# A two-block transformer kernel: the second norm's first steps made beside the first block's output projection, and weight totals asked for one group later

## What is computed

```
x = layer_norm(x, ln_in_g, ln_in_b)
h = einsum('bsd,de->bse', x, w_in[l])
...                                    # the three mixers: ya, yb, yc
y = einsum('bse,ed->bsd', concatenate([ya, yb, yc], -1), w_out[l])
x = layer_norm(DEEPNORM_ALPHA * x + y, post_ln_g[l], post_ln_b[l])      # x1

h = rmsnorm(x, norm_pre_g)             # y = xf * rsqrt(mean(xf*xf) + eps) * g
z = einsum('bsd,de->bse', h, w_in)
...                                    # rope, three dilated window attentions, gates, a convolution
y = einsum('bse,ed->bsd', mixed, w_out)
x = x + rmsnorm(y, norm_post_g)
```

## Time and profile before

| | |
|---|---|
| median of 3 runs | 2297.74 us (2291.33 to 2300.5) |
| profiled execution | 2291.84 us |
| its span, first to last instruction | 2289.7 us |
| mean granted TensorE clock | 0.962 |
| busy: PE, DVE, ACT, POOL | 91%, 61%, 40%, 40% |
| PE idle ahead of line 236, five single waits | 2.67, 2.72, 2.76, 2.67, 4.34 us |
| last projection matmul to first dense matmul of the second norm | 920.35 to 955.32 us |

### The profile page before, as it was taken

How to read it: one execution, slowest core, us unless ns; L and a number is a source line. 1 busy time by engine, 2 the same in 40 slices (tenths; PEclk the granted TensorE clock), 3 DMA queues, 4 the chain that set the end, 5 groups by cost and what they waited for, 6 DMA issues and landing times.

```text
span 2289.7 us, 43310 instructions
## 1 busy us (share of the span) xinstructions
PE 2082.4 (91%) x16228; PEld 1525.7 (67%) x16228; DVE 1394.7 (61%) x3507; ACT 923.1 (40%) x1981; POOL 906.7 (40%) x1004
## 2 busy tenths in 40 slices
PE   5999999997898999499999999999988888887998
PEld 3545868886787888488644444656877766666786
DVE  7614949765897444773376772213179999994422
ACT  3323333222796000232233431211179999883111
POOL 4311333363422999332111211211132888983222
PEclk9999999998899999799999999999999999997999
DMA  5441321346633232442344431321156787674552
GB/s 180 134 110 57 108 80 44 92 142 201 154 80 107 79 109 98 156 135 66 115 118 137 117 116 49 117 73 55 49 123 161 195 197 185 169 220 135 161 172 90
DMA packets 285536, 279.95 MB, mean 122 GB/s; under 512 B 39712, under 2 KB 237216, under 8 KB 285072
## 3 DMA queue, kind: packets, MB, share of 16 engines
q1 hardware_dynamic: 281280, 271.08, 41.1%
q0 software_dynamic: 1680, 5.51, 0.6%
q10 hardware_dynamic: 2368, 0.60, 0.1%
HBM read 171.22 MB, written 93.31 MB: 116 GB/s over the span
## 4 chain that ended last, share of the span: by engine, by line
PE 27%; DVE 16%; issue 4%; ACT 2%; POOL 2%; DMA 2%; SPq 1%; DVEq 0%; ACTq 0%; POOLq 0%
PE bank L172 19%; PE bank L2507 7%; DVE s2m L2357 6%; DVE p2l L2363 4%; DMA qr<-qf 1%; DVE qf L1801 1%; SPq L1830 1%; ACT s2sh L1781 1%; DVE qr L1799 1%; DVE s2sl L1804 1%; DVE qf L1798 1%; DVE ob L2369 1%; PE bank L2302 1%; POOL qs L2399 0%; ACT p2r L2336 0%
## 5 line engine op out<-in xcount | busy, mean ns | idle before, releaser
L172 PE MATMUL bank<-xh,w2l 128*128 128x512 f16 x640 | 244.7, 382 | 0.0
L172 PE MATMUL bank<-xh,w2h 128*128 128x512 f16 x640 | 244.5, 382 | 0.0
L172 PE MATMUL bank<-xl,w2h 128*128 128x512 f16 x640 | 244.5, 382 | 0.0
L172 PE MATMUL bank<-w1h,xh 128*128 128x256 f16 x768 | 212.6, 277 | 3.0 <-DVE s1st L918 3.0
L172 PE MATMUL bank<-w2h,xh 128*128 128x256 f16 x768 | 211.3, 275 | 2.0 <-issue 2.0
L2302 PE MATMUL bank<-ident,p2r 128*128 128x128 f32 x900 | 165.9, 297 | 51.9 <-DVE p2l L2363 45.7
L172 PE MATMUL bank<-w1l,xh 128*128 128x256 f16 x768 | 212.5, 277 | 0.0
L172 PE MATMUL bank<-w1h,xl 128*128 128x256 f16 x768 | 212.4, 277 | 0.0
L172 PE MATMUL bank<-w2h,xl 128*128 128x256 f16 x768 | 211.2, 275 | 0.0
L172 PE MATMUL bank<-w2l,xh 128*128 128x256 f16 x768 | 211.2, 275 | 0.0
L2302 PEld LDWEIGHTS bank<-ident,p2r 128*128 128x128 f32 x900 | 97.4, 145 | 108.5 <-DVE p2l L2363 105.7
(11 more groups left out here) (345 smaller groups left out, 5643.1 us busy)
## 6 DMA issues: line engine op xcount, KB each, us to landing
scr_part<-ob SPq DMA_DIRECT2D x48, 264.0 KB, 3.2
cm<-scr_part SPq DMA_DIRECT2D x48, 264.0 KB, 4.7
v<-scr_v SPq DMA_DIRECT2D x192, 65.0 KB, 2.6
w2r<-in_w_in SPq DMA_DIRECT2D x12, 1024.0 KB, 6.4
qr<-qf SPq DMA_DIRECT2D x192, 64.0 KB, 2.0
ax<-in_x SPq DMA_DIRECT2D x16, 512.0 KB, 5.3
xr<-in_x SPq DMA_DIRECT2D x16, 512.0 KB, 4.4
bx<-scr_x SPq DMA_DIRECT2D x16, 512.0 KB, 6.2
```

The lines of the kernel that those rows point to most:

```text
L172: ins = nc.tensor.matmul(dst, x, y, start=k == 0 and m == 0, stop=k == n - 1 and m == 2)
```

## The change

Four things. (1) The second norm's gain scale, the load, statistics and scaling of its first four row tiles, and its first weight chunk's load, square, total and scale are made in `project_stage`, between tiles 5 and 15, in tiles of their own (`rows2`, `raw2`, `junk2`). ACT scales the rows, not DVE. (2) The stores of x1 are left out of the take-over; row loads wait for the stores of their own rows. All engines take over first and then begin. (3) In both norms the totals of chunks 2 and 3 stand one dense group later. (4) In the gate stage the total stands behind the fourth tile of a chunk, not the second, and the scaling one tile later. Chunk 2 of the second norm no longer shares its buffer with chunk 0, so its load doesn't wait for it. The core of the diff:

```diff
-        handed_over = hand_over() if late else ()
+        handed_over = hand_over(ahead["stores"]) if late else ()
...
-        if late:
-            sb(f"{tag}pad", [128, 17000], scope=scope)
...
-        work = [("wide",), ("load", 0)]
+        work = [] if late else [("wide",), ("load", 0)]
...
             if g == 1:
-                work += [("load", 2), ("total", 2)]
+                work.append(("load", 2))
+            if g == 2:
+                work.append(("total", 2))
...
-        work += [("consts",), ("load", 3), ("total", 3)]
-        work += [("group", 2, 0), ("scaled", 3)] + [("group", 2, g) for g in range(1, 4)]
+        work += [("consts",), ("load", 3)]
+        work += [("group", 2, 0), ("total", 3), ("group", 2, 1), ("scaled", 3), ("group", 2, 2), ("group", 2, 3)]
...
-                elif x_ready is not None:
-                    sp.wait_ge(*x_ready[t])
+                if late:
+                    sp.wait_ge(*ahead["stored"][4 * g + t])
...
-                    pe.wait_ge(*d_sc.at(4 * g + 4))
+                    pe.wait_ge(*(ahead["scaled"] if late and g == 0 else d_sc.at(4 * (g - off) + 4)))
...
         def dve_program():
-            if not keep:
-                dve_most()
-                dve_widest()
+            take_over(dve)
+            if not late:
+                dve_scale(0)
                 dve_widened()
-            dve_scale(0)
-            if keep:
-                dve_widened()
-            take_over(dve)
...
         def sp_program():
-            sp_fetch(0)
             take_over(sp)
-            wts.sp_load(0)
+            if not late:
+                sp_fetch(0)
+                wts.sp_load(0)
             wts.sp_load(1)
...
     # project_stage
+            if n == 8:
+                wide_bank = tbk.take(d_wd.at(5))
+            if n == 13:
+                total_bank = tbk.take(d_wt.at(1))
+        def sp_ahead(n):
+            if n == 6:
+                nc.sync.dma_start(raw2[:], ...).then_inc(*w_in.up(16))
+            if 8 <= n < 12:
+                t = n - 8
+                sp.wait_ge(*x_out[t].at(16))
+                nc.sync.dma_start(rows2[t][:], x1[128 * t:128 * t + 128, :]).then_inc(*n_in[t].up(16))
+        def dve_ahead(n):            # behind dve_residual(n + 2)
+            if n == 5:
...                                  # four small operations on the gain
+            elif n == 8:
+                dve.wait_ge(*p_wd.at(1))
+                nc.vector.tensor_scalar(whole, wide_bank[0][:, 0:1], 1e-30, None, ALU.max).then_inc(*d_wd.up())
+            elif n == 11:
...                                  # two small operations
+            if 10 <= n < 14:
+                t = n - 10
+                dve.wait_ge(*n_in[t].at(16))
...                                  # bn_stats x2, bn_aggr of rows2[t]
+            elif n == 14:
...                                  # three small operations
+            if n == 13:
+                dve.wait_ge(*p_wt.at(1))
+                nc.vector.tensor_scalar(size2[:, 0, 1:2], total_bank[0][:, 0:1], 1e-30, None, ALU.max).then_inc(*d_wt.up())
+        def act_ahead(n):            # behind ACT's copies of tile n
+            if n == 10:
+                act.wait_ge(*w_in.at(16))
+                nc.scalar.activation(junk2[:], raw2[:], ACT.Square, accum_out=size2[:, 0, 0:1]).then_inc(*a_ws.up())
+            elif n == 15:
+                act.wait_ge(*g_nx.at(1))
+                for t in range(4):
+                    nc.scalar.activation(rows2[t][:], rows2[t][:], ACT.Identity, scale=rs2[:, t:t + 1]).then_inc(*a_nx.up())
+        def pool_ahead(n):           # behind POOL's power of tile n
...                                  # n == 10: three small operations; n == 13: five; n == 14: one power of four columns
     # PE, round n, behind pe_turn(n + 1)
+                if n == 7:
+                    nc.tensor.matmul(wide_bank[0][:, 0:1], ones_[:], own, start=True, stop=True).then_inc(*p_wd.up())
+                if n == 12:
+                    nc.tensor.matmul(total_bank[0][:, 0:1], ones_[:], size2[:, 0, 0:1], start=True, stop=True).then_inc(*p_wt.up())
...
     # gate_stage
-                    if len(tiles) % 8 == 2 and first + n + 1 < len(wts.chunks):
+                    if len(tiles) % 8 == 4 and first + n + 1 < len(wts.chunks):
...
-                if m % 8 == 1 and x["n"] in total_bank:
+                if m % 8 == 3 and x["n"] in total_bank:
                     wts.pe_total(first + x["n"] + 1, *total_bank[x["n"]])
...
-                if m % 8 == 4 and first + m // 8 + 1 < len(wts.chunks):
+                if m % 8 == 5 and first + m // 8 + 1 < len(wts.chunks):
                     wts.act_scale(first + m // 8 + 1)
...
-                if m % 8 == 2 and x["n"] in total_bank:
+                if m % 8 == 4 and x["n"] in total_bank:
                     wts.dve_total(first + x["n"] + 1, total_bank[x["n"]][0])
```

More of the change, by code:

```diff
@@ L184, in __init__ @@
             self.lo = sbs(f"{tag}l", 2, [128, 8, 256], FH, scope)
-            self.size = sb(f"{tag}z", [128, len(chunks), 4], scope=scope)
+            self.size = sb(f"{tag}z", [128, len(chunks), 4], scope=scope) if first is None else first["size"]
             self.un = [un[:, block, n:n + 1] for n in range(len(chunks))]
@@ L192, in __init__ @@
             at, dma_at = [None, self.a_w.n, self.d_w.n, self.g_w.n], [x.n for x in self.dma]
[L193 to L196, removed]
+            done = 0 if first is None else 1
+            self.summed = [(self.a_n, self.a_n.n + n + 1 - done) for n in range(len(chunks))]
+            self.added = [(self.p_t, self.p_t.n + n + 1 - done) for n in range(len(chunks))]
+            self.total = [(self.d_t, self.d_t.n + n + 1 - done) for n in range(len(chunks))]
+            self.scaled = [(self.g_u, self.g_u.n + 5 * (n - done) + 5) for n in range(len(chunks))]
+            if first is not None:
+                self.scaled[0] = first["scaled"]
             self.landed, self.by_act, self.half, self.ready = [], [], [], []
+            self.first = first
             for n, c in enumerate(chunks):
-                dma_at[n % 2] += 16 * len(c["cols"])
+                dma_at[n % 2] += 16 * len(c["cols"]) if n or first is None else 0
                 at[1] += 1
-                self.landed.append((self.dma[n % 2], dma_at[n % 2]))
+                self.landed.append((self.dma[n % 2], dma_at[n % 2]) if n or first is None else first["landed"])
                 self.by_act.append((self.a_w, at[1]))
@@ L211, in __init__, with raw_of @@
             self.spent, self.read = {}, {}
+        def raw_of(self, n):
+            return self.first["raw"] if n == 0 and self.first is not None else self.raw[n % 2]
         def sp_load(self, n):
@@ L215, in sp_load @@
                 return
-            if n > 1:
+            if n > (1 if self.first is None else 2):
                 sp.wait_ge(*self.ready[n - 2])
@@ L313, in norm_stage @@
         d_wd, d_gs, g_wd, g_xh, p_wd = sem("d_wd"), sem("d_gs"), sem("g_wd"), sem("g_xh"), sem("p_wd")
-        if late:
-            sb(f"{tag}pad", [128, 17000], scope=scope)
         block = 1 if late else 0
         own, whole = wide[:, 2 * block:2 * block + 1], wide[:, 2 * block + 1:2 * block + 2]
-        wts.widened = d_gs.at(1)
+        wts.widened = ahead["widened"] if late else d_gs.at(1)
+        fitted_at = ahead["fitted"] if late else d_gs.at(2 if shift is None else 3)
+        off = 1 if late else 0
         splits = [wts.chunks[n]["kind"][0] == "f" for n in range(3)]
@@ L329, in norm_stage @@
         p_vt, a_vf = sem("p_vt"), sem("a_vf")
-        n_most = 2 if shift is None else 3
+        n_most = 0 if late else 3
         for k, n in enumerate(valued):
             wts.read[n] = d_bd.at(n_most + 3 * k + 1)
-        xs = sbs(f"{tag}x", 4, [128, D], F32, scope)
+        xs = ahead["rows"] if late else sbs(f"{tag}x", 4, [128, D], F32, scope)
         xf = sbs(f"{tag}f", 4, [128, 512], F32, scope)
@@ L365, in norm_stage @@
             if item[0] == "wide":
-                wide_bank = bk.take(g_wd.at(0) if False else d_wd.at(3))
+                wide_bank = bk.take(d_wd.at(3))
             elif item[0] == "total":
@@ L371, in norm_stage @@
                     turn_bank[item[1], k] = bk.take(a_turn.at(8 * item[1] + k + 1))
-                    if item[1] == 0 and k == 1:
+                    if item[1] == 0 and k == 1 and not late:
                         total_bank[0] = bk.take(wts.total[0])
@@ L460, in pool_power @@
             r_out = rs_in[:, 4 * g:4 * g + 4] if keep else rs[:]
-            pool.wait_ge(*d_st.at((14 if keep else 15) * (g + 1)))
+            pool.wait_ge(*d_st.at((14 if keep else 15) * (g + 1 - off)))
             pool.wait_ge(*POWER)
@@ L484, in pe_program @@
                         ins.then_inc(*p_tr.up())
-                        if g == 0 and k == 1:
+                        if g == 0 and k == 1 and not late:
                             wts.pe_total(0, *total_bank[0])
@@ L621, in dve_program @@
```

(6 more changed lines are left out.)

109 lines of the change are left out of this document (85 added, 24 removed).

## The result

The changed kernel takes 2257.69 us (median of 4 runs, 2255.5 to 2258.43) against 2296.85 of the kernel before (4 runs, 2291.33 to 2300.5) beside it: ratio 0.983, 95% interval 0.981 to 0.985. That is 39.2 us by the medians. The two profiled executions lie closer together, 2291.84 and 2258.43 (spans 2289.7 and 2256.6), 33.4 us, since that of before is among its kernel's fastest and that of after its kernel's slowest.

The account below looks back on a forecast made before the run. TensorE's holes were taken as the bound: the hole behind the projection and five waits at totals. 14.0 + 22.0 = 36.0 us off the profiled 2291.84 gives 2255.8, 2261.7 from the median; forecast 2259, range 2250 to 2274.

Parts of the forecast that it names:

- the hole: Between last projection matmul and first dense matmul of the second norm, 35 us before; 16.85 us of gain in the sum.
- What bounds it: TensorE is full otherwise in these stages, so time taken out of its holes shortens the span if nothing else ends later.
- Part 1, GpSimd, VectorE, ScalarE, SP: Projection tiles 5 to 15: waits and pauses hide the added work; GpSimd lags 1.5 us at most, gone by the end.
- Part 1, TensorE: Projection: two totals borrow transpose banks, delaying tiles 10 and 15, so TensorE ends 2.85 us later (bounds 0.3 and 6).
- Part 1, the turns: Behind the projection: turns begin about 930.0, casts and subtractions end 941.2; first dense group 941.3, not 955.32: 14.0 us.
- Part 2: Both norms and the gate stage: totals asked later hide their waits, 22.0 us gained (bounds 15.2 and 22.0).
- The five waits: TensorE's waits at the one-column total for ScalarE's sum of squares, 2.67, 2.72, 2.76, 2.67 and 4.34 us: 15.2 us.
- the four spells at half clock: Behind four of TensorE's five waits at the totals, half clock costs 1.7 us each, 6.8 us in all.
- Late burst: Behind the projection: shared transfers land chunk 1 in 12.5 to 15 us, losing 5.7 us of gain, 2265 us; 17%.
- One sign that the prediction named for being wrong: At the second norm's start: ScalarE waiting for chunk 1 behind its turns would show the prediction wrong; no size given.
- Returned waits: Norms: if turned rows end last, three of four waits return as waits for VectorE, 13 us, 2272 us; 14%.
- Slower: Projection from tile 10: banks freed only after the same tile's power, 52 us lost, net 16 slower, 2311 us; 4%.

Follow-up runs that it names:

- the totals alone: The kernel before with only the totals of both norms and the gate stage asked later, no work moved into the projection: 2269.23 us, ratio 0.990.
- the six others that keep its projection: Changed kernel with totals early again (2278.67 us), two take-over semaphores (2250.69), row loads delayed (2253.67), x1 stores awaited (2260.98), gate totals later (2290.21, 2338.95).
- the kernel with two waits: The changed kernel, but each engine waits at the take-over for two semaphores instead of some thirty: 2250.69 us, one time.
- rows held back: The changed kernel, but the four row loads of the second norm's second group wait until weight chunk 1 has landed: 2253.67 us, one run.
- stores waited for: The changed kernel, but the stores of x1 are waited for at the take-over again: 2260.98 us, one run.
- reads moved: The changed kernel with VectorE's reads of two one-column sums moved in the projection, the gain's later, the chunk's earlier: 2262.78 us, one run.
- the two of the gate stage: The changed kernel with the gate stage's totals behind a chunk's sixth tile, or behind its eighth: 2290.21 and 2338.95 us, one run each.

## Why the prediction held

The forecast was 2259 and the median is 2257.69. Its sum, 36.0 us, lies between the 33.4 of the profiled executions and the 39.2 of the medians. That it came within 1.3 us is in part luck: those two measures of the gain differ by 5.8 us, and the sum had one term too large (the hole, by 1.4) and lacked another (the rope stage, 3.2), both below. Step by step:

**What bounds it.** Right: time taken out of TensorE's holes came off the span, stage by stage.

**Part 1, GpSimd, VectorE, ScalarE, SP.** Right. GpSimd's additions are gone before its last power, which waits 2.57 us for VectorE (916.88). The rows are scaled from 909.49 on, 8 us earlier than the 918 of the prediction, which is that stage's own shift.

**Part 1, TensorE.** 2.85 us were predicted and 2.1 measured. From the first transposes to VectorE's end are 197.4 us without the hand-over (before, and the totals alone), 199.6 in the changed kernel, 199.7 to 200.5 in the six others that keep its projection: 2.2 to 3.1 more. The size held; its make-up, one wait of 1.7, one of 0.85 and 0.3 for both totals, was 0.9 to 1.3, 0.5 to 0.8 and some 0.24 for each total.

**Part 1, the turns.** The step that failed is "ScalarE issues its store and begins to turn at about 930.0", 0.55 us behind VectorE's end at 929.45. No row stands behind the 0.55. The take-over has some thirty waits, and going through them cost 1.2 us, which the kernel with two waits gave back. That is the missing size in the hole: 16.85 predicted, 15.5 measured. Behind it the estimate of casts and subtractions was right: 11.3 us from the first turn (930.0 to 941.3), 11.5 measured (922.52 to 933.99). Its make-up was not: the casts, put at 1.23 us each, took 0.80 for the first four and 1.32 for the last four.

**Part 2.** 22.0 us predicted; 22.4 in the changed kernel by the table, 23.4 with the totals alone. The five waits are 15.2 us. The granted clock of before shows the four spells at half clock: 3.4 us each, from 136.0, 1003.0, 1067.9 and 1385.3, which is 1.7 us lost in each, 6.8, as counted. The 1.4 left of 23.4 stands close around the waits, 0.3 at each: a wait of 4.34 us puts 4.72 between the starts of TensorE's instructions (1379.54 to 1384.26), where 0.21 is usual, and the next matmul starts 0.25 behind the total, where the changed kernel has 0.14. The room was there: no wait for turned rows or for a split took their place. The one long wait left in the second norm, 4.50 us for VectorE in the second turn (953.80), stood in before as well (4.61).

**What the sum lacked.** The rope stage lost 3.2 us and nothing in the change touches it. TensorE waits there for a bound that VectorE makes when the last value store has landed. First three rows of the changed kernel, then two of before:

```profile
1086.66 2.29 DVE L1860 TENSOR_REDUCE qwm<-w2r 128x8 f32<-128x2048 f32 x1 [4.18 <-DMA scr_v<-bvo]
1089.40 0.58 PE L1870 MATMUL bank<-qbd,ones 128*128 128x1 f32 x2 [3.25 <-DVE qbd L1864]
1089.85 0.59 PE L173 MATMUL bank<-xh,w2h 128*128 128x512 f16 x1
...
1117.80 0.38 PE L1761 MATMUL bank<-qbd,ones 128*128 128x1 f32 x2 [2.13 <-DVE qbd L1755]
1119.58 0.63 PE L172 MATMUL bank<-xh,w2h 128*128 128x512 f16 x1
```

The wait is 1.1 us longer than in before. The half clock at it lasts 6.8 us (1089.0 to 1095.9 by the granted clock) against 3.4 (1119.1 to 1122.5), which is another 1.7, and two later waits of the stage (0.50 and 2.51 against 0.32 and 2.17) make the other 0.5. In the kernel with two waits TensorE waits 3.10 us there and goes on at full clock; with the rows held back it waits 2.17 us and falls to half clock. Seven kernels are alike from the second norm's first dense group through this stage (the changed one, two waits, rows held back, stores waited for, reads moved, and the two of the gate stage). Four of them lose 2.3 to 3.2 us here against before and three gain 0.1 to 0.5, so I put it down to scatter between executions. That explains why the sum overshoots the profiled pair, not why the medians differ by more than the sum.

**Rivals.** Late burst: chunk 1 landed 8.5 us behind its issue and not 12.5 to 15, and under the turns and subtractions that costs nothing. One sign that the prediction named for being wrong did show, in small: ScalarE waits 0.65 us for chunk 1 behind its turns (929.79), but its total at 931.85 is still 2.0 us ahead of the end of the last subtraction. Returned waits: none. Slower: tile 10 made 4.3 us late by hand cost that once; the loop didn't close.

## What to carry to other kernels

A step that a pass makes at a stage's border is worth moving ahead when its engines stand still there for another reason, and its price is then read at the banks it borrows, not at its own durations. A take-over that waits for everything is itself work (1.2 us on ScalarE, 0.9 on GpSimd, 0.4 on SP here): wait for the one step that stands behind the rest. A request moved later to hide its wait needs the whole way from request to use, the queue of each engine on it included: in the gate stage two tiles later brought 6 us, four lost 22.

## What the runs showed of the hardware

- Some thirty satisfied semaphore waits held ScalarE for 1.2 us and GpSimd for 0.9.
- Small GpSimd operations grow when VectorE is at work on large tiles. With the total behind the eighth tile, these two take 2.34 us each, beside two convolution passes of VectorE, and 0.23 and 0.26 at four of the six changes of chunk:

```profile
1382.69 4.74 DVE L2035 SCALAR_TENSOR_TENSOR acc<-uin,cw,acc 128x2048 f32<-128x2048 f32 x2
1382.79 2.34 POOL L259 TENSOR_SCALAR size<-size 128x1 f32<-128x1 f32 x1
1385.22 2.34 POOL L261 TENSOR_SCALAR un<-size,wide 128x1 f32<-128x1 f32 x1
```

  That is why two of the six waits are 15 us and not 10. The Trainium skill (SBUF — State Buffer, section SBUF: two separate sides) describes the port pair that the two share as a lock that the first to start keeps for its whole instruction. The trace agrees: VectorE's passes end at 1385.04 and 1387.43, the two operations 0.1 us behind them.
- A megabyte chunk lands 6.9 to 8.5 us behind its issue at this place, 5.6 in the earlier trace rows. What shares the DMA engines with it explains most of that: its packets start over 3.7 us in before and 4.5 with the rows held back, where nothing else moves, but over 6.1 to 6.5 where the store or the rows lie among them; the first starts 1.0 to 1.1 us behind the issue, or 2.0 where the store goes ahead. Why it is 4.5 and not 3.7 stays open.
- Half clock behind a wait of TensorE comes and goes: behind 2.67 us at 72.23 none follows in before, behind 2.13 us (1117.80) and 2.72 (135.49) it does; behind 3.10 us none follows in the kernel with two waits. A spell lasted 3.4 us in these places, 6.8 in the changed kernel's rope stage.
